# Expert down-projection weights loaded as two 64-row halves with 32 KB rows, nine pairs of sixteen

## What is computed

```
def moe(x, router_w, router_b, w1, b1, w2, b2):
    ...
    for e in range(N_EXPERTS):
        gu = xt @ w1[e] + b1[e]                       # w1[e]: 1024 x 2048
        gate = jnp.minimum(gu[:, :D_FF], SWIGLU_LIMIT)
        lin = jnp.clip(gu[:, D_FF:], -SWIGLU_LIMIT, SWIGLU_LIMIT)
        glu = gate * jax.nn.sigmoid(SWIGLU_ALPHA * gate)
        out = (glu * (lin + 1.0)) @ w2[e] + b2[e]     # w2[e]: 1024 x 1024
        acc = acc + combine[:, e:e + 1] * out
```

## Time and profile before

| | us |
|---|---|
| median of 3 runs | 1020.68 |
| lowest, highest | 1020.45, 1022.2 |
| the profiled execution, its own time | 1020.11 |
| its span in the trace | 1018.4 |
| mean granted TensorE clock in it | 0.987 |

### The profile page before, as it was taken

The page is one execution under the profiler, slowest core; times in us unless marked ns, Lnnn a source line. Parts: engine busy times, 40 slices in busy tenths (PEclk is TensorE's granted clock), DMA queues, the critical chain, the costliest instruction groups (busy, mean ns, idle before and its releaser), DMA issues.

```text
span 1018.4 us, 12840 instructions
## 1 busy us (share of the span) xinstructions
PE 950.4 (93%) x5422; PEld 427.7 (42%) x5422; DVE 295.8 (29%) x517; ACT 167.2 (16%) x354; POOL 74.5 (7%) x62
## 2 busy tenths in 40 slices
PE   8999999999998998989899898889899899998996
PEld 7999444343332433333243333324243334343332
DVE  5897622131312122221212222121312213131212
ACT  5355612011010101011020101002010101010012
POOL 5986000000000000000000000000000000000000
PEclk9999999999999999999999999999999999999998
DMA  9979999999999999999999999999999999999994
GB/s 321 325 296 424 368 423 432 433 426 433 425 436 425 437 432 426 432 425 434 428 434 431 431 432 424 438 423 436 427 433 431 425 438 421 434 424 434 421 419 182
DMA packets 31584, 420.60 MB, mean 413 GB/s; under 512 B 4262, under 2 KB 5062, under 8 KB 12721
## 3 DMA queue, kind: packets, MB, share of 16 engines
q1 hardware_dynamic: 31083, 418.97, 97.5%
q10 hardware_dynamic: 462, 1.10, 0.3%
HBM read 418.75 MB, written 1.49 MB: 413 GB/s over the span
## 4 chain that ended last, share of the span: by engine, by line
issue 89%; PE 9%; DMA 1%; DVE 0%; ACTq 0%; POOLq 0%; POOL 0%; DVEq 0%
PE psum L787 2%; PE psum L788 2%; PE psum L789 2%; PE psum L821 1%; PE psum L820 1%; PE psum L819 1%; DMA rows_all<-in_x_sample 1%; PE psum L706 0%; PE psum L775 0%; PE psum L796 0%; PE psum L698 0%; POOLq L86 0%; POOL rms L1982 0%; PE psum L849 0%; PE psum L765 0%
## 5 line engine op out<-in xcount | busy, mean ns | idle before, releaser
L997 PE MATMUL psum<-ring,rows_all 128*64 128x512 f32 x2012 | 460.9, 607 | 41.0 <-DMA ring<-in_exp_w 40.6
L997 PEld LDWEIGHTS psum<-ring,rows_all 128*64 128x64 f32 x2012 | 138.9, 139 | 317.8 <-issue 258.6
L1014 PE MATMUL psum<-ring,rows_all 128*64 128x512 f32 x896 | 198.0, 595 | 12.2 <-DMA ring<-in_exp_w 12.2
L1014 PEld LDWEIGHTS psum<-ring,rows_all 128*64 128x64 f32 x896 | 67.2, 137 | 134.1 <-issue 134.1
L1436 ACT ACTIVATE rows_all<-rows_all 128x512 f32<-128x512 f32 x32 | 20.1, 630 | 528.8 <-DVE rows_all L1791 528.8
L1808 DVE SCALAR_TENSOR_TENSOR y_low<-psum,gate_of,y_high 128x512 fp32r<-128x512 f32 x32 | 23.7, 751 | 243.3 <-ACT y_high L1444 243.1
L1791 DVE TENSOR_SCALAR rows_all<-psum 128x512 f32<-128x512 f32 x32 | 22.1, 692 | 196.2 <-PE psum L997 196.2
L1780 DVE TENSOR_TENSOR rows_all<-rows_all,psum 128x512 f32<-128x512 f32 x56 | 36.0, 684 | 121.1 <-PE psum L1064 121.1
L1984 POOL TENSOR_TENSOR rms<-rms,half 128x3 f32<-128x3 f32 x1 | 0.8, 849 | 910.0 <-DVE rms L1931 910.0
L1444 ACT ACTIVATE y_high<-psum,gate_of 128x512 fp32r<-128x512 f32 x32 | 22.0, 688 | 214.6 <-PE psum L1014 188.1
L890 PEld LDWEIGHTS psum<-place,x_thirds 128*128 128x128 bf16 x744 | 46.6, 97 | 13.0 <-issue 13.0
(11 more groups left out here) (270 smaller groups left out, 764.6 us busy)
## 6 DMA issues: line engine op xcount, KB each, us to landing
ring<-in_exp_w SPq DMA_DIRECT2D x53, 4096.0 KB, 30.5
ring<-in_exp_w SPq DMA_DIRECT2D x72, 2048.0 KB, 25.4
ring<-in_exp_w SPq DMA_DIRECT2D x18, 1024.0 KB, 25.6
ring<-in_w_in SPq DMA_DIRECT2D x3, 2048.0 KB, 19.8
ring<-in_w_out SPq DMA_DIRECT2D x1, 4096.0 KB, 13.0
ring<-in_exp_w SPq DMA_DIRECT2D x2, 1536.0 KB, 17.7
ring<-in_exp_w SPq DMA_DIRECT2D x5, 512.0 KB, 19.8
held<-in_exp_w SPq DMA_DIRECT2D x1, 2048.0 KB, 11.8
```

The lines of the kernel that those rows point to most:

```text
L997: last = mm(psum[c * SLOTS:(c + 1) * SLOTS, bank, :], gathered_t[:, 4 * kk + j, e, :], weights, start=False, stop=(kk == 1 and j == 3), sk ...
L1014: last = mm(psum[e * SLOTS:(e + 1) * SLOTS, 4 + c, :], h_t[:, 4 * i + j, e, :], ring_w2[:, slot, e, j, c * BANK:(c + 1) * BANK], start=Fal ...
```

## The change

For pairs 1 to 9 (`wide=True`) a unit of w2 holds one whole expert: partition p has rows 8p to 8p + 7, 32 KB in one run. The unit is loaded by two loads, of partitions 0 to 63 and of partitions 64 to 127 (`load_wide`), 64 x 32 KB = 2048 KB each. So a pair's w2 is four loads of 2048 KB as before, with half as many rows of twice the length. The second product (`wide_product`) waits for both units, goes through both together and raises `used` by 2 at its very end. The hidden activations are permuted by eight in place of four (`run`), and are turned by 32 small products of 64 columns (`turn_wide`) in place of eight of 128. Pairs 0 and 10 to 15 stay as they are.

Beside it: the four `seed` products move from TensorE to ScalarE (`write_seed`, copies into PSUM); SyncE waits for a part of the last weights before it issues the final gain's loads; the store of the samples is split in four, two on SyncE and two on ScalarE.

```
             def load_w2(pair, kk, e, slot):
                 ...
+            def load_wide(pair, e, slot):
+                rows = exp_w2[0][bass.ds(pair * 2 + e, 1)].rearrange("e (p j) n -> p (e j n)", j=8)
+                for a in range(2):
+                    own = slice(a * SLOTS, (a + 1) * SLOTS)
+                    nc.sync.dma_start(ring_flat[own, slot], rows[own]).then_inc(landed[slot], 16)
...
+                    elif wide:
+                        load_wide(pair - 1, i, slot)
                     else:
                         for e in range(2):
                             load_w2(pair - 1, i, e, slot)
...
-                with nc.sync.Fori(1, HALF - 2) as m:
+                with nc.sync.Fori(1, WIDE) as m:
                     h = reg(nc.sync, r * HALF + m, ROUNDS * HALF)
-                    load_period(h, 0, m * 2)
-                    load_period(h, 1, m * 2 + 1)
+                    load_period(h, 0, m * 2, wide=True)
+                    load_period(h, 1, m * 2 + 1, wide=True)
+                h5 = reg(nc.sync, r * HALF + WIDE, ROUNDS * HALF)
+                load_period(h5, 0, WIDE * 2, wide=True)
+                load_period(h5, 1, WIDE * 2 + 1)
...
-            load_last(reg(nc.sync, more * HALF + HALF, ROUNDS * HALF))
+            h8 = reg(nc.sync, more * HALF + HALF, ROUNDS * HALF)
+            load_last(h8)
+            sp.wait_ge(third_landed, 4 * h8)
             nc.sync.dma_start(gain_final, final_norm_g[None, :].to_broadcast([P, D])).then_inc(g_final_landed, 16)
...
+            def turn_wide(h, b, bank=6):
+                for e in range(2):
+                    pe.wait_ge(h_ready, 4 * h + 2 * b + e - 1)
+                    for j in range(8):
+                        for a in range(2):
+                            own = slice(a * SLOTS, (a + 1) * SLOTS)
+                            last = mm(psum[own, bank + e, j * SLOTS:(j + 1) * SLOTS],
+                                      gate_act[:, e, j * SLOTS:(j + 1) * SLOTS], ident[:, own],
+                                      start=True, stop=True, skip_group_check=True)
                     last.then_inc(h_t_ready, 1)
...
+            def wide_product(h, b, at_unit):
+                slots = [(at_unit + e) % UNITS for e in range(2)]
+                pe.wait_ge(h_t_read, 4 * h + 2 * b)
+                for e in range(2):
+                    pe.wait_ge(landed[slots[e]], arrivals(h, at_unit + e))
+                for j in range(8):
+                    for c in range(YN):
+                        for e in range(2):
+                            last = mm(psum[e * SLOTS:(e + 1) * SLOTS, 4 + c, :], h_t[:, j, e, :],
+                                      ring_wide[:, slots[e], j, c * BANK:(c + 1) * BANK],
+                                      start=False, stop=(j == 7), skip_group_check=True)
+                        if j == 7 and c < YN - 1:
+                            last.then_inc(y_ready, 1)
+                last.then_inc(used, 2)
...
-                if end:
-                    seed(0)
                 half_product(h8, h_t, 1, 1, 1, 4)
                 pe.wait_ge(h_t_read, 4 * h8)
                 add_b2(h8, 0, y_bank=0)
-                if end:
-                    seed(1)
+                pe.wait_ge(seeds_written, 3 * h8)
...
+            def write_seed(j):
+                c, t = TILES[j]
+                A(psum[:, LAST_BANKS[j], :], x_acc[:, t, c * BANK:(c + 1) * BANK], ACT.Copy).then_inc(seeds_written, HALF)
```

More of the change, by code:

```diff
@@ L563, in load_first, with load_period @@
                     load_w1(pair, i, i)
-            def load_period(h, b, pair, last=False, kept=False, half=False):
+            def load_period(h, b, pair, last=False, kept=False, half=False, wide=False):
                 first = 4 if b else -2
@@ L686, in _ @@
                 nc.sync.dma_start(y_prompt[0][t * P:(t + 1) * P, :], x_norm[:, t, :]).then_inc(stored, 16)
-            sp.wait_ge(stored, 16 * 4)
+            sp.wait_ge(final_dve, 3)
+            for q in (2, 3):
+                nc.sync.dma_start(sample_rows[:, q * QUARTER:(q + 1) * QUARTER],
+                                  samples_out[q * NS:(q + 1) * NS]).then_inc(stored, 16)
+            sp.wait_ge(stored, 16 * 7)
             sp.wait_ge(cache_stored, 16 * 4)
@@ L945, in turn_hidden @@
                     last.then_inc(h_t_ready, 1)
+            def turn_wide(h, b, bank=6):
[7 more added lines that the diff above has]
+                                      start=True, stop=True, skip_group_check=True)
+                    last.then_inc(h_t_ready, 1)
             def turn_caches():
@@ L1081, in spread_tile, with period @@
                 return_rows(b, j, 6 + j % 2, True, True).then_inc(spread, 1)
-            def period(h, b, first=False, spreads=True, final=False, kept=None, half=None):
+            def period(h, b, first=False, spreads=True, final=False, kept=None, half=None, wide=False):
                 direct = first and isinstance(h, int)
@@ L1091, in period @@
                     pe.wait_ge(gt_read, 16 * h + 8 * b)
-                if not (first or second):
+                if wide:
+                    turn_wide(h, b)
+                elif not (first or second):
                     turn_hidden(h, b)
@@ L1215, in round_of @@
                 period(h0, 1, spreads=False)
-                with nc.tensor.Fori(1, HALF - 2) as m:
+                with nc.tensor.Fori(1, WIDE) as m:
                     h = reg(nc.tensor, r * HALF + m, ROUNDS * HALF)
-                    period(h, 0)
-                    period(h, 1)
+                    period(h, 0, wide=True)
+                    period(h, 1, wide=True)
+                h5 = reg(nc.tensor, r * HALF + WIDE, ROUNDS * HALF)
+                period(h5, 0, wide=True)
+                period(h5, 1)
                 h6 = reg(nc.tensor, r * HALF + HALF - 2, ROUNDS * HALF)
@@ L1444, in high_y, with period @@
                     A(y_high[:, c, :], psum[:, y_bank + c, :], ACT.Copy, scale=gate_of[:, 1 - b:2 - b]).then_inc(y_high_ready, 1)
-            def period(h, b, first=False, final=False):
+            def period(h, b, first=False, final=False, wide=False):
                 second = isinstance(h, int) and h + b == 1
@@ L1456, in period @@
                     copy_hidden_t(h, b + 1, h_t_last, bank=0)
+                    act.wait_ge(h_ready, 4 * h + 2 * b + 2)
+                    write_seed(0)
+                    write_seed(1)
                 if not final:
@@ L1484, in round_of @@
                 period(h0, 1)
-                with nc.scalar.Fori(1, HALF - 2) as m:
+                with nc.scalar.Fori(1, WIDE) as m:
                     h = reg(nc.scalar, r * HALF + m, ROUNDS * HALF)
-                    period(h, 0)
-                    period(h, 1)
+                    period(h, 0, wide=True)
+                    period(h, 1, wide=True)
+                h5 = reg(nc.scalar, r * HALF + WIDE, ROUNDS * HALF)
+                period(h5, 0, wide=True)
+                period(h5, 1)
                 h6 = reg(nc.scalar, r * HALF + HALF - 2, ROUNDS * HALF)
@@ L1520, in _ @@
             act.wait_ge(final_dve, 3)
-            nc.scalar.dma_start(y_sample.rearrange("b t (q n) -> q (b t) n", q=4), samples_out).then_inc(stored, 16)
+            for q in (0, 1):
+                nc.scalar.dma_start(sample_rows[:, q * QUARTER:(q + 1) * QUARTER],
+                                    samples_out[q * NS:(q + 1) * NS]).then_inc(stored, 16)
         @block.vector
@@ L1786, in copy_back, with activate @@
                 V.tensor_scalar(back[:, b, :], psum[:, 6, 0:T], 0.0, None, ALU.is_gt).then_inc(back_read, 1)
-            def activate(h, b, at_used):
+            def activate(h, b, at_used, run=4):
                 for e in range(2):
@@ L1810, in low_y, with period @@
                                            op1=ALU.subtract).then_inc(y_low_ready, 1)
-            def period(h, b, pair, first=False, spreads=True, final=False):
+            def period(h, b, pair, first=False, spreads=True, final=False, wide=False):
                 at_first = 12 * h + (5 if b else 1 if first else -1)
@@ L1829, in period @@
                     V.tensor_copy(pick_b2[:], picked(pair - 1)).then_inc(picked_b2, 1)
-                activate(h, b, 12 * h + (8 if b else 4 if first else 2))
+                activate(h, b, 12 * h + (8 if b else 4 if first else 2), run=8 if wide else 4)
                 if final:
@@ L1911, in round_of @@
                 period(h0, 0, 0, first=True, spreads=False)
-                period(h0, 1, 1, spreads=False)
-                with nc.vector.Fori(1, HALF - 2) as m:
+                period(h0, 1, 1, spreads=False, wide=True)
+                with nc.vector.Fori(1, WIDE) as m:
                     h = reg(nc.vector, r * HALF + m, ROUNDS * HALF)
-                    period(h, 0, m * 2)
-                    period(h, 1, m * 2 + 1)
+                    period(h, 0, m * 2, wide=True)
+                    period(h, 1, m * 2 + 1, wide=True)
```

(3 more changed lines are left out.)

30 lines of the change are left out of this document (21 added, 9 removed).

## The result

The changed kernel takes 1226.26 us (median of 4 runs, 1222.93 to 1233.22); the kernel before took 1021.04 us in the runs beside it. The ratio is 1.202, 95% interval 1.1997 to 1.2043, so the change costs 206 us (204 to 209). The forecast was 1185 us with a range of 1060 to 1210: the direction and the main mechanism (half rate for half of the partitions) hold, the size was too small by 41 us.

What follows compares the result with a forecast made beforehand. Loads were taken to bound the kernel, with TensorE close behind. The sum was 1020.11 + 175.5 - 10 - 1 = 1184.6 us, and with the median 0.57 higher the forecast was 1185 us, range 1060 to 1210.

Steps and rivals of the forecast that it cites:

- Longer rows: w2 loads: 32 KB runs move no faster than 16 KB runs, 0 us, within 2 us either way.
- The halves: w2 loads of 64 partitions run at half rate: 19.5 us more per pair, 175.5 us for nine; lower bound nothing.
- the 1.45 of the bias loads: Middle bound for w2's split loads, from narrow loads' packet times: 8.8 us per pair, 79 us for nine.
- What engines out of step give back: w2 loads: engines sharing a way but in different halves run at full speed meanwhile, -10 us, bounds 0 and -36.
- Slots come free later: w2 slots released at the second product's end: queued w1 loads cover it, 0 us, +18 at most.
- Rival 4: w2 at half rate with gaps on top, +18 us or more: 1205 to 1220 us, chance 0.05.
- TensorE's waiting for both units and its turning: Second product 7.1 us later, turning 1.1 us more per pair, both covered by waits for loads: 0 us.
- The end: Last products: taking seeds off TensorE mostly lengthens its waits for loads, -1 us, bounds 0 and -2.
- No sharing (1): Rival: split w2 loads run on at 430 GB/s as if whole, 1018 to 1022 us, chance 0.13.
- No drift (2): Rival on w2 loads: engines drift apart and stay so, 1040 to 1140 us, about 1100, chance 0.17.
- Rival 3: w2 at full rate, but waiting for both units or late slots cost 0.5 to 2 us per pair: 1025 to 1040, chance 0.03.

Runs made afterwards that it cites:

- whole16: The changed kernel with each wide w2 unit in two loads of 128 partitions x 16 KB, split by columns: 1026.52 us, ratio 1.0054.
- whole32: The changed kernel with each wide w2 unit in one load of 128 partitions x 32 KB: 1027.89 us, ratio 1.0061.
- quarters: The changed kernel with each wide w2 unit in four loads of 32 neighbouring partitions: 1222.19 us, ratio 1.1976.
- twoq: The changed kernel with lower halves issued by SyncE and upper halves by GpSimd, behind the same waits: 1260.97 us, ratio 1.237.
- evenodd: The changed kernel with a wide unit's two loads naming even and odd partitions, 64 each: 1027.18 us, ratio 1.0053.
- narrow16: The kernel before, with only its w2 loads in pairs 1 to 9 split by partitions, not by expert: 1221.07 and 1223.57 us, ratio 1.1967.
- nowide: The changed kernel with all wide=True set to wide=False, leaving only the edits beside it: 1021.47 us, ratio 1.0001.
- late: The kernel before, with only both w2 units waited for and released together in pairs 1 to 9: 1027.09 us, ratio 1.0062.
- whole32_awake: whole32 with four products nobody reads ahead of the wait for w2: 1021.23 us, ratio 1.0005.
- awake26: The changed kernel with 26 products nobody reads ahead of the wait for w2: 1222.46 us, ratio 1.1978.

## Why the prediction was off

The account, worked out from experiments that each hold one part: the halves alone +201 us (199 to 203), the late slots alone +6.4 (4.9 to 7.9), the edits beside it 0, together 207; the whole change measured 206. Three terms of the sum failed, two of them by their size or sign (the half rate with its borders, and what the engines' offset gives back) and one that was put at 0 (the late slots).

**Longer rows, 0 us.** Right. whole16 and whole32 are the same.

**The halves.** The choice among three bounds was right: not nothing, not the 1.45 of the bias loads, but the half. The bias loads understated the loss; that their rests are the reason, as the prediction had it, was not tested. What the page "SBUF — State Buffer" of the Trainium skill says in its section "Door 1: The DMA port swizzle", that partitions 0 to 63 reach 8 of the 16 ports and 64 to 127 the other 8, the rates of the runs bear out: 210 to 215 GB/s while the two halves are loaded in turn, and 210 for quarters. The section "Can I just issue two DMAs to hit both halves?" of that page of the Trainium skill (the prediction calls it the next one) says that they serialize, and twoq agrees: a second queue gave no gain. The same section of the Trainium skill says that only one transfer spanning all 128 partitions hits all ports; if that is meant of the number of partitions, evenodd does not bear it out: its loads name 64 each, and the kernel takes 1027.18 us, as with whole loads.

**The size of that term, 19.5 us per pair.** This is the first step that failed, by its size: it measured 22.3 us, 201 in place of 175.5. The packet records of two traces say where the rest lies, since in narrow16 and in the kernel before, w2 in the wide pairs comes in packets of 16 KB and w1 in packets of 32 KB. Summed up and divided by 16 engines, the 16 KB packets of the kernel before took 367.0 us and those of narrow16 548.2; the 32 KB packets 516.3 and 538.0; all others 115.0 and 115.3, and of the span 20.1 and 20.3 us are left over. So w2 itself costs 181 us, 20.1 per pair, near the 19.5 of the sum. The other 22 us, 2.4 per pair, are w1's: 469 of its packets in narrow16 took more than 1.25 us, up to 2.8, where the mean before is 1.22, and nearly all of these lie at the borders between w1 and w2. In the changed kernel the stretches from 453 to 455 and 493 to 497 us are slower than either side:

```profile
453.00:455.00 2.00, 2.00 (x12) 0.63 (x10) 0.96 (x3) 0.00 (x0) 0.00 (x0) 1.00 0.72 147
...
493.00:495.00 2.00, 0.00 (x0) 0.00 (x0) 0.00 (x0) 0.00 (x0) 0.00 (x0) 0.50 0.71 147
495.00:497.00 2.00, 0.00 (x0) 0.00 (x0) 0.00 (x0) 0.00 (x0) 0.00 (x0) 0.50 0.85 197
```

A stretch of 2 us holds few packets of 32 KB, so single numbers of these stretches are rough (the 2 us ahead of the first moved 492 GB/s).

**What engines out of step give back, -10 us** (0.3 x 4 x 9 is 10.8; the sum took 10). The second step that failed, wrong in sign: I counted the offset as time in which partners are in different halves. Nothing was given back on w2, and w1 lost 22 us at the borders. An engine that is early into w2, or late out of it, takes a share of a way that another still needs for w1: w1's packets of about twice their usual time fit with that. Which engine met which was not traced, so this cause is argued; shown is whose packets lost the time and where.

**Slots come free later, 0 us.** The third step that failed: 6 us. It named the condition, a product at the lower clock after a longer rest, with up to 2 us per pair, but left it to a rival (chance 0.05) and priced the cover at 5.3 us with a product of 14.2 us. Even with whole loads the rest before the product grew to some 5 us, the clock fell, and the product took some 16 us; the next loads went out 1.6 us later than at the full clock, and the queue moved less behind them (398 GB/s in those 14 us). In the changed kernel's own trace the time left over beside the packets is 28.2 us, against 20.1 before and 20.3 in narrow16, so it has such gaps too. Rival 4 (half rate and gaps, 1205 to 1220) was the case that came, by its mechanism, though the time lies above its range as well.

**TensorE's waiting for both units and its turning, 0 us.** Right for TensorE's own time; what the waiting cost came through the slots.

**The end, -1 us.** 0 (nowide). The freed time became a longer wait for loads: the products of the last pairs that wait for parts of a unit waited 3.1 us there (L1080), 1.1 us before (L1031).

**Rivals 1 to 3.** No sharing (1) is out. No drift (2): the rate of w2 does not climb from pair to pair; stretches of 80 us at 380 and at 780 us move much the same:

```profile
380.00:460.00 80.00, 53.80 (x343) 21.87 (x341) 11.84 (x21) 5.49 (x13) 0.00 (x0) 0.83 1.00 310
...
780.00:860.00 80.00, 52.02 (x339) 21.44 (x339) 12.77 (x22) 6.11 (x14) 0.00 (x0) 0.83 0.97 301
```

Rival 3 (no sharing, but late slots, 1025 to 1040) is what whole32 and evenodd are: 1027 us.

With 22.3 in place of 19.5, nothing given back and nothing gained at the end, the sum would have been 1020.1 + 201 + 0.6 = 1222, and with the late slots 1228; measured were 1226.

## What to carry to other kernels

The DMA engines were as busy with the slow loads as with the quick ones, so look at what they move and not at how busy they are. Here loads of 32 or 64 neighbouring partitions ran at half the rate of loads of 128, and the splits that cost nothing were those in which each part reaches across all partitions (by columns, or every second partition). A slow load also costs its neighbours: part of the loss stood in the packets of w1 next to it. If several buffers are released together, work out how much is queued behind them, with the product's time at the lower clock if the engine rests before it. Where a load of the shape in question is missing from a trace, a short one may understate what a full queue will show, as the bias loads did here.

## What the runs showed of the hardware that I had not expected

- Two loads of 64 partitions each, the even and the odd, run as fast as one of 128 (1027.18 and 1027.89 us), while w2 in a lower and an upper half takes twice as long.
- Splitting the halves over two queues made it worse: 1260.97 us against 1226.26, with stretches at 141 GB/s.
- In the traces of whole16, whole32, evenodd and late, rests of 4 to 6.8 us before the second product went with 15.3 to 17.0 us for it; in whole32_awake rests of 1.0 to 1.4 us went with 13.95 us. Around 3 us there are both: 13.95 us after 3.33 in evenodd, 15.65 us after 2.92 in awake26. The stretch at the product's start shows the lower of the two levels, 0.50, which is 1.2 GHz, and the product was slow in its first part only:

```profile
415.00:419.00 4.00, 3.90 (x10) 1.39 (x12) 0.00 (x0) 0.00 (x0) 0.00 (x0) 0.50 1.05 451
419.00:423.00 4.00, 4.00 (x18) 1.35 (x16) 0.00 (x0) 0.00 (x0) 0.00 (x0) 0.90 1.09 467
423.00:427.00 4.00, 4.00 (x22) 1.51 (x20) 0.00 (x0) 0.00 (x0) 0.00 (x0) 1.00 0.91 393
```

These are stretches of the changed kernel; the clock stands before the last two columns.
